# Spreading softmax reciprocals over rows by two DMAs through DRAM instead of by PE transposes

## The reference, cut to what matters

```python
s = jnp.einsum('bqhd,bkhd->bhqk', q_i, k, preferred_element_type=jnp.float32) * scale
s = logit_fn(s, b_i)
pr = jax.nn.softmax(s, axis=-1).astype(v.dtype)
return jnp.einsum('bhqk,bkhd->bqhd', pr, v)
...
mixed = (o_c * jax.nn.silu(g_c)) @ fox_w_out[l]
```

## Time and profile before

| | us |
|---|---|
| median of 3 runs | 1892.64 (1892.39 to 1895.32) |
| the profiled execution | 1891.66 |
| its span, first to last instruction | 1889.9 |

### The profile page before, as it was taken

The page is one execution under the profiler, slowest core; times in us unless marked ns, Lnnn a source line. Parts: engine busy times, 40 slices in busy tenths (PEclk is TensorE's granted clock), DMA queues, the critical chain, the costliest instruction groups (busy, mean ns, idle before and its releaser), DMA issues. The chain is left out here.

```text
span 1889.9 us, 31611 instructions
## 1 busy us (share of the span) xinstructions
PE 1728.8 (91%) x12560; PEld 1610.2 (85%) x12560; DVE 948.3 (50%) x1810; ACT 836.7 (44%) x1708; POOL 109.6 (6%) x64
## 2 busy tenths in 40 slices
PE   5999788898998888999989999999989999889898
PEld 5999787787888777989989999898777777789898
DVE  5454475303777773262455444321077787733531
ACT  4432233314888882151352323322178888711410
POOL 0000000000122220000000000000002122100000
PEclk9999899999999999999989999999999999999999
DMA  5045357626546654111223344443265656250211
GB/s 191 23 160 173 112 149 204 180 69 166 155 121 177 167 137 179 51 52 33 90 87 103 124 134 125 136 137 95 84 168 135 151 125 152 68 190 29 73 62 40
DMA packets 179523, 227.14 MB, mean 120 GB/s; under 512 B 13209, under 2 KB 148649, under 8 KB 179377
## 3 DMA queue, kind: packets, MB, share of 16 engines
q1 hardware_dynamic: 178080, 221.31, 40.9%
q0 software_dynamic: 864, 2.95, 0.5%
q10 hardware_dynamic: 432, 0.85, 0.1%
HBM read 153.22 MB, written 77.62 MB: 122 GB/s over the span
## 5 line engine op out<-in xcount | busy, mean ns | idle before, releaser
L1642 PE MATMUL m_acc<-g_area,g_a_hi 128*128 128x256 f32 (+1 forms) x2560 | 479.2, 287 | 10.1 <-DVE g_area L209 5.6
L1642 PEld LDWEIGHTS m_acc<-g_area,g_a_hi 128*128 128x128 f32 x2560 | 404.2, 193 | 10.4 <-DVE g_area L209 5.8
L1642 PE MATMUL m_acc<-g_area,g_a_lo 128*128 128x256 f32 (+1 forms) x1280 | 366.1, 286 | 0.0
L1642 PEld LDWEIGHTS m_acc<-g_area,g_a_lo 128*128 128x128 f32 x1280 | 244.9, 191 | 0.0
L662 PE MATMUL pa_acc<-g_area,g_a_hi 128*128 128x256 f32 (+2 forms) x1024 | 208.0, 300 | 15.9 <-DVE g_area L209 15.9
L1642 PE MATMUL t_acc<-g_area,g_a_hi 128*128 128x256 f32 x1024 | 189.6, 285 | 5.1 <-DVE g_area L209 5.1
L662 PEld LDWEIGHTS pa_acc<-g_area,g_a_hi 128*128 128x128 f32 x1024 | 166.7, 195 | 16.4 <-issue 16.4
L209 DVE TENSOR_TENSOR g_area<-g_w_raw,g_area 128x2048 fp32r<-128x2048 f32 (+5 forms) x55 | 112.0, 2050 | 125.8 <-ACT g_area L203 125.8
L1642 PEld LDWEIGHTS t_acc<-g_area,g_a_hi 128*128 128x128 f32 x1024 | 160.3, 192 | 5.3 <-DVE g_area L209 5.3
L662 PE MATMUL pa_acc<-g_area,g_a_lo 128*128 128x256 f32 (+2 forms) x512 | 151.3, 296 | 0.0
L1642 PE MATMUL t_acc<-g_area,g_a_lo 128*128 128x256 f32 x512 | 145.4, 284 | 0.0
(11 more groups left out here) (231 smaller groups left out, 3281.3 us busy)
## 6 DMA issues: line engine op xcount, KB each, us to landing
g_w_raw<-in_fox_w_in SPq DMA_DIRECT2D x16, 1024.0 KB, 6.0
g_area<-f_q SPq DMA_DIRECT2D x48, 256.0 KB
g_area<-f_k SPq DMA_DIRECT2D x48, 256.0 KB
g_w_raw<-in_ab_w_in SPq DMA_DIRECT2D x10, 1024.0 KB, 5.7
ab_v<-s_v SPq DMA_DIRECT2D x16, 512.0 KB, 3.6
g_area<-s_q SPq DMA_DIRECT2D x32, 256.0 KB
g_w_raw<-in_pe_gate_w SPq DMA_DIRECT2D x8, 1024.0 KB, 5.2
f_v<-m_pr SPq DMA_DIRECT2D x32, 256.0 KB, 2.8
```

What stands on the lines that cost most here:

```text
L1642: last = nc.tensor.matmul(dst, a[:, k, t * P:(t + 1) * P], w[:, k0 + k, 0:n], start=(k == 0 and a is m_hi and w is w_hi), stop=(k == kt - ...
```

## The change

A whole head's sums are inverted by one DVE instruction (`invert` returns for u < 3, and takes all eight tiles at u = 3). SP then writes the 128 x 8 reciprocals to a row of 1024 floats in DRAM (`s_inv`), in steps of 4 bytes, waits until that write has landed, and reads the row back, broadcast to the 64 rows of that head's half of `far`. It does so for head hd-2 after it has issued the loads of head hd, and for the last but one head before the early load of the next weights. PE does no spreading transposes, `take_far` copies the product alone (64 x 256 instead of 64 x 512), and POOL waits for the two broadcasts of its pair instead of for `far_done`. The last head of a stage keeps the transposes and a reciprocal per unit. The semaphore `rows_stored` is made at the top instead of in the first stage.

```diff
+    s_inv = dram("s_inv", [FH, S])
...
-            total = sp.sb("total", [P, 4, 2])
-            inverse = sp.sb("inverse", [P, 4, 2])
+            total = sp.sb("total", [P, 2, NT])
+            inverse = sp.sb("inverse", [P, 2, NT])
...
+                    def spread_inverse(hd):
+
+                        b, m = hd % 2, hd // 2
+                        sync.wait_ge(inverted, hd + 1)
+                        sync.dma_start(s_inv[hd].rearrange("(t q) -> q t", q=P), inverse[:, b, :]).then_inc(inv_out[b], 16)
+                        wait(sync, gi_done, m - 1)
+                        sync.wait_ge(inv_out[b], 16 * (m + 1))
+                        sync.dma_start(far[64 * b:64 * b + 64, m % 2, :, 1, :],
+                                       s_inv[hd:hd + 1].rearrange("o (u n) -> o u n", u=NU).to_broadcast([64, NU, 2 * P]))\
+                            .then_inc(inv_in[b], 16)
...
                         if hd % 2 == 0:
                             load_gate(hd // 2)
+                        if hd >= 2:
+                            spread_inverse(hd - 2)
+                    spread_inverse(heads - 2)
...
                         if 4 <= s < TILES + 4 and s % 2 == 0:
-                            spread_sums((s - 4) // 2)
-                            times_v((s - 4) // 2, False)
+                            uu = (s - 4) // 2
+                            wait(pe, o_done, uu - 1)
+                            if uu >= NU * (heads - 1):
+                                spread_sums(uu % NU)
+                            times_v(uu, False)
...
+                        if t == 0:
+                            wait(act, inverted, s // NT - 1)
...
-                        act.wait_ge(spread, uu + 1)
+                        if last:
+                            act.wait_ge(spread, u + 1)
...
-                        nc.scalar.activation(far[64 * b:64 * b + 64, m % 2, uu % NU], pv[64 - 64 * b:P - 64 * b, uu % 2],
+                        what = slice(0, 2 if last else 1)
+                        nc.scalar.activation(far[64 * b:64 * b + 64, m % 2, u, what], pv[64 - 64 * b:P - 64 * b, uu % 2, what],
                                              ACT.Copy).then_inc(far_done, 1)
...
                     def invert(uu):
+                        hd, u = divmod(uu, NU)
+                        b, m = hd % 2, hd // 2
+                        tiles = slice(0, NT)
+                        if hd == heads - 1:
+                            tiles = slice(2 * u, 2 * u + 2)
+                        elif u < NU - 1:
+                            return
                         dve.wait_ge(exped, 2 * uu + 2)
-                        wait(dve, spread, uu - 3)
-                        nc.vector.reciprocal(inverse[:, uu % 4, :], total[:, uu % 4, :]).then_inc(inverted, 1)
+                        wait(dve, inv_out[b], 16 * m)
+                        nc.vector.reciprocal(inverse[:, b, tiles], total[:, b, tiles]).then_inc(inverted, 1)
...
-                        pool.wait_ge(far_done, 2 * NU * (m + 1))
+                        for b in range(2):
+                            pool.wait_ge(inv_in[b], 16 * (m + 1))
```

More of the change, by code:

```diff
@@ L225, in build @@
     bias_wrote = G.sem("bias_wrote")
-    skewed = G.sem("skewed")
+    skewed, rows_stored = G.sem("skewed"), G.sem("rows_stored")
     def stage_ab():
@@ L280, in stage_ab @@
             made, chain, scaled_cols = sp.sem("made"), sp.sem("chain"), sp.sem("scaled_cols")
-            rows_made, rows_stored = sp.sem("rows_made"), sp.sem("rows_stored")
+            rows_made = sp.sem("rows_made")
             x_sq, x_inv, x_root, x_made = sp.sem("x_sq"), sp.sem("x_inv"), sp.sem("x_root"), sp.sem("x_made")
@@ L1009, in stage_attention @@
             ones = sp.sem("ones")
+            inv_out, inv_in = [sp.sem("inv_out0"), sp.sem("inv_out1")], [sp.sem("inv_in0"), sp.sem("inv_in1")]
             last_gi, last_gated, last_hi = sp.sem("last_gi"), sp.sem("last_gated"), sp.sem("last_hi")
@@ L1082, in turn_p, with spread_sums @@
                             last.then_inc(pieces_turned, 1)
-                    def spread_sums(uu):
-                        wait(pe, o_done, uu - 1)
-                        pe.wait_ge(inverted, uu + 1)
+                    def spread_sums(u):
+                        pe.wait_ge(inverted, heads + u)
                         for i in range(2):
-                            last = nc.tensor.transpose(pv[:, uu % 2, 1, i * P:(i + 1) * P],
-                                                       inverse[:, uu % 4, i:i + 1].to_broadcast([P, P]), ident[:])
+                            last = nc.tensor.transpose(pv[:, u % 2, 1, i * P:(i + 1) * P],
+                                                       inverse[:, (heads - 1) % 2, 2 * u + i:2 * u + i + 1].to_broadcast([P, P]),
+                                                       ident[:])
                         last.then_inc(spread, 1)
@@ L1132, in exp @@
                                              scale=-1.0 if chk else 1.0,
-                                             accum_out=total[:, s // 2 % 4, s % 2:s % 2 + 1]).then_inc(exped, 1)
+                                             accum_out=total[:, s // NT % 2, t:t + 1]).then_inc(exped, 1)
                     def evacuate(s):
@@ L1145, in take_far @@
                     def take_far(uu):
-                        b, m = uu // NU % 2, uu // (2 * NU)
+                        b, m, u = uu // NU % 2, uu // (2 * NU), uu % NU
+                        last = uu >= NU * (heads - 1)
                         act.wait_ge(pv_done, uu + 1)
-                        act.wait_ge(spread, uu + 1)
+                        if last:
+                            act.wait_ge(spread, u + 1)
                         if uu % (2 * NU) == 0:
                             wait(act, out_lo, m - 1)
-                        nc.scalar.activation(far[64 * b:64 * b + 64, m % 2, uu % NU], pv[64 - 64 * b:P - 64 * b, uu % 2],
+                        what = slice(0, 2 if last else 1)
+                        nc.scalar.activation(far[64 * b:64 * b + 64, m % 2, u, what], pv[64 - 64 * b:P - 64 * b, uu % 2, what],
                                              ACT.Copy).then_inc(far_done, 1)
@@ L1225, in gate_last @@
                             dve.wait_ge(in_g[m % 2], 16 * (m // 2 + 1))
+                            dve.wait_ge(inv_in[0], 16 * NPAIR)
                             wait(dve, gated, m)
```

## The result

The changed kernel takes 2055.43 us (median of 4 runs, 2053.02 to 2058.23) against 1892.52 us (4 runs, 1889.93 to 1895.32): a ratio of 1.0861 [1.0839, 1.0883], 163 us slower. The forecast was 1877 us with a range up to 1898. The profiled execution took 2058.23 us with a span of 2056.4.

A forecast was written before the change was run, and what follows sets the result against it. PE looked like the bound, but in fox the chain from tile 4 on was taken to be ACT and DVE. Savings of 19.0 us less 3.6 us of POOL waits gave 15.4 us: 1877.2 us, range 1862 to 1898.

The forecast's parts named there:

- The new chain to POOL: POOL's `gi` after write and broadcast: starts 6.6 us later, hidden in mla and fox, 3.6 us of waits in chk.
- x: Landing of the reciprocals' write in DRAM, counted from the issue of v; taken as 4.9 us, between 3.4 and 5.4.
- rows 10: Profile rows at 16:17 us: DMA engines 99% busy moving 16 GB/s, read as the price of single words.
- rival B: Write lands late, ACT waits at `give` in all 14 pairs, formula 14x - 72.9 us; typically 1900 to 1913; chance 0.20.
- The broadcast: Read of the reciprocals into `far`, 256 KB in rows of 1 KB: lands in 2.8 us, like another 256 KB transfer.
- A delay of a few us costs nothing: SP queue: q and k loads behind the blocking wait have most of a head until needed, so zero cost.
- The savings: Attention stages, from ACT's narrower copy and PE's dropped transposes: mla 5.1, chk 5.9, fox 8.0, together 19.0 us.
- The copy's 0.21 us: ACT's far copy narrowed from 593 to 381 ns: 0.21 us less per unit, 25.2 us of ACT over 120 units.
- The transposes: PE's spreads, 0.22 us a unit: one per head counts in mla, the others are hidden by waits.
- Rival A: PE is the bound after all, so all its saved slots show, 26.4 us: 1866 us; chance 0.15.
- rival C: Savings hidden by waits for scores; only the copy behind exp of tile 7 shows, 6.3 less 3.6: 1890 us; chance 0.15.
- DVE and the moved weight load: Three reciprocals a head fewer on DVE, and SP's early weight load moved to head 15's tile 1: both counted zero.

The follow-up runs named there:

- e3: Changed kernel without both DMAs and without transposes for all but the last pair, POOL multiplying the gate by itself (division left out there): 1882.03 us, ratio 0.9938.
- e4: Kernel before, transposes kept, far copy taking the product alone in all but the last two heads, division left out there: 1878.9 us, ratio 0.9922.
- e1: Changed kernel with reciprocals written as 128 runs of 32 bytes instead of 1024 single words, read back in another order: 1882.5 us, ratio 0.9944.
- e11: Changed kernel with reciprocals turned on PE and written as eight 512-byte runs, ACT copying the pair after tile 2's exponentials: 1878.5 us, ratio 0.9929.
- e2: Changed kernel with ACT copying a finished pair at tile 7 of the next head instead of tile 1: 2017.25 us, ratio 1.0648.
- e6: Changed kernel with its single-word write, but 64 different rows of x read back instead of the broadcast, division left out: 2046.38 us.
- e9: Changed kernel with POOL instead of SP waiting for the write and issuing the broadcast: 2094.44 us, ratio 1.1057.
- e9b: Changed kernel with POOL waiting and issuing the broadcast, and ACT copying the pair at tile 7 instead of tile 1: 2010.35 us, ratio 1.0615.
- e14: Changed kernel writing 1024 neighbouring single words in the other order, each partition its eight consecutively; row read from x, division left out: 2015.27 us.

## Why the prediction was wrong

- **The failed step is "The new chain to POOL": the landing of the write.** It took x = 4.9 us, from the 5.0 us of a read in the mirrored shape. Measured: 15.0 in ab and 12.8 in fox. That row is a read of 1024 neighbouring words, one by one in the same order, and it was no upper bound for the store of them. The prediction named the missing row ("without an upper row") and then drew its range as if 8 were far out. Its other sign, rows 10, pointed elsewhere: there the DMA engines were 99% busy, while the slow store leaves them at 0.00 for six microseconds.
- **The mechanism was rival B's, and its formula held from 4 to 15 us.** For the measured landings it gives 159 us of waits where the trace has 166, and in the table it stays within 9 us in every stage. B's price (1900 to 1913) was wrong only by the size put into it. Less the 12.5 us saved (e3, e4) the waits leave some 9 of the 163 us. I put them down to the granted clock of 0.50 to 0.54 during and after a stall, which no step had; no run isolates it.
- **The broadcast**: 2.8 us taken, 3.7 to 3.9 measured when the write is short, 5.5 when it is long. This alone is worth 1 us in x: with the fast write of e1 the waits were 4.3 us, near the 3.6 of the prediction.
- **"A delay of a few us costs nothing" for SP** was right for a few us (e1, e11) and wrong for 14: e2 has 107 us of PE waiting for loads. The step compared the delay with the slack of one load, and not the queue's own loop (20.5 us on average) with the head's 17.
- **The savings**: 19.0 us predicted, 17.6 of it for the 28 heads that e3 changes; measured 13.2. The copy's 0.21 us is exact, and of its 112 places in e4 (23.5 us) 12 us show for 15.8 predicted (the 17.6 without mla's 8 x 0.22). The transposes, 1.8 us predicted, gave about 1 by the stages, which the medians don't bear out. Rival A (all PE slots show, 26.4 us) fell; rival C (6.3 us) fell too.
- DVE and the moved weight load: at nothing, and no wait of after speaks against it. e1, in which only the failed term is put right, came out at 1882.5, 11.7 us faster than its own runs of before, for 15.4 predicted.

## What to carry to other kernels

Before a store goes out in single neighbouring words, turn it on the chip so that it leaves in runs; here the read of the same shape gave no bound for it, and where no row of a trace bounds a transfer from above, the range has to stay open on that side. When a queue is made to wait for a round trip through DRAM, add up its whole loop per iteration and hold that against the loop of the engines, not the delay against one load's slack. And after the experiment that removes a wait, look for the one behind it: two limits that hang on the same landing hide each other.

## What the runs showed of the hardware

- A store of 4-byte words side by side in DRAM landed in 10.5 to 14.9 us (1024 words; after, e2, e6, e9, e9b, e14), 11.6 to 12.9 (512 words); a read of as many in the same shape in 5.0; the same 1024 words 16, 32 or 64 bytes apart in 4.7 to 5.5; as 128 runs of 32 bytes in 3.6 to 4.0.
- While it is under way the DMA engines show no work for six microseconds, and the 512 KB load issued just before it lands in 8.3 to 9.6 us (5.8 to 10.0 over all runs with such a store) for 3.4 to 3.6.
- In a stall of PE of 13 us the granted clock was still 1.00 at its start and 0.50 (1.2 GHz) in its later part, and 0.54 in the six microseconds after the stall.
- Open: why half the words cost nearly as much as all, by what mechanism neighbours are slow (or whether it is the short stretch that they cover), what such a store takes without a load just ahead of it, and why the broadcast lands later from POOL's queue (5.3 to 9.8 us) than from SP's (5.5).
